# Projection and attention in one block, attention's setup among the last u products, MLP's last tile by halves

## The chip, the cores and the metric

The kernel runs on one core of one Trainium2 chip. The time is the device time of one execution in microseconds (us); of several executions the median is given. Lower is better. The five engines of a core are TensorE (PE in the rows, its weight loads PEld), VectorE (DVE), ScalarE (ACT), GpSimd (POOL) and SyncE (SP), which here only issues DMAs. They run side by side, each in its own program order, and wait for one another through semaphores.

## What is computed

One layer of a diffusion backbone, in float32, on 1024 latent tokens and 128 context tokens of width 1024:

```python
h = rmsnorm(x, norm1) * (1 + scale1) + shift1
proj = h @ w_in
q_a, kv_a, k_r, u = jnp.split(proj, [256, 384, 416], axis=-1)
q = (rmsnorm(q_a, q_norm) @ w_qb).reshape(B, S, N_HEADS, QK_DIM)      # 8 heads of 64 + 32
ckv = rmsnorm(kv_a, kv_norm)
kv = (keys_ckv @ w_kvb).reshape(B, K, N_HEADS, QK_NOPE_DIM + V_HEAD_DIM)
attn = mla_attend(q_nope, q_rope, k_nope, keys_kr, v)                 # softmax over latent and cached keys
pooled = pool_mix(u, w_pool, pool_scale)                              # windowed means of u, 4 groups
x = x + gate1 * (jnp.concatenate([attn, pooled], axis=-1) @ w_o)
h2 = rmsnorm(x, norm2) * (1 + scale2) + shift2
x = x + gate2 * (jnp.square(jax.nn.relu(h2 @ w1)) @ w2)               # 1024 -> 4096 -> 1024
```

A last `rmsnorm(x, final_norm)` gives y. Scale, shift and gate come from `silu(c) @ w_ada + b_ada`, once for the latent tokens and once for the context. ckv and the rotary key of the context tokens are outputs too.

## The kernel before

Every large product is made of three: each float32 operand is split into a high part (ScalarE, `ACT.Copy` into fp32r) and the rest (VectorE or GpSimd, a subtraction), and high·high, high·low and low·high add up in one PSUM bank. So each tile goes through PE, ACT and DVE in turn, and of the eight PSUM banks some are always being split.

The program has three blocks. At the border of two blocks all engines meet at a barrier.

**project_phase** (from L184). Nine token tiles of 128. `STEPS` numbered steps; tables such as `A_AT`, `U_AT` and `M_AT` say what each engine does at which step. `U_AT` places the 16 products `project_u` (L763, written m = 0 to 15: 4 blocks of tiles by 4 groups of columns of u), `M_AT` the products `mix` (L790) that follow them three steps later. Between these two, one m passes `read_u` on ACT, `windows` on POOL, `pooled` on DVE, `pooled_high` on ACT and `pooled_low` on DVE; after `mix`, `mixed` on ACT. The sums for the first gate (`gate_sums`, L798) multiply 128x128 weights by `sel`, which has two columns; they stand at step 26 on PE, behind the last u product (step 24) and between the last mixes. The queries' input `qnT`, the compressed keys `ckvT` and the rotary key rows `krT` are left for the next block. `small_hi` and `small_lo` make them, the context tile's last (step 24).

**attention_phase** (from L835). First a setup with nothing else beside it: the weights of heads 0 and 1 are split (L1076, L997), PE makes head 0's three key pieces (L1318) and three query pieces (L1307), then the values of all heads for ten key tiles (`V`, L1418, 30 products of 512 columns), with five banks in turn. ACT and DVE split the keys, put the rotary rows `krT` into `kT` for both buffers (L1134, L1246), turn the queries (`turn_query`, L1191), fill `ropeq` with ones (L1249) and split the values (L1144, L1257). Then a loop runs over `u` = 0 to 67: 64 units (8 heads by 8 query tiles), each with `scores(u)` (nine products of 384 columns, L1337) on PE, `maximum(u)` on DVE (L1210, L1212), `exponent(u)` on ACT (L1110) and, one to two units later, transposes (L1351) and products with `V` (L1362), four for a pair of units in flight. Sides of the loop are the next head's keys and queries (`SIDE_AT`), sums for three later modulations (`ADA_AT` on DVE and POOL, and `MOD_AT` on PE: L1381, again products by `sel`, four times in the loop) and the context's own attention. `scores(u)` for u > 0 waits until the exponent of u-1 has read the banks. Banks 0 to 2 hold scores, bank 6 the products with `V`, banks 3, 4, 5 and 7 are a ring for all the rest.

**closing_phase** (from L1511). The output projection (L1694), and then the MLP in three blocks of 3 token tiles by 32 slices of the hidden width: `up` (L1951), ReLU and square, `down_tile` (L1959). Behind the last slice PE makes the last three tiles one by one, each with 12 products of 512 columns in two banks. For each, DVE multiplies by the gate in two halves (L1900), POOL adds to x in two halves (`residual`, L1763), ACT takes the sum of squares (L1831), POOL makes the inverse root (L1767, L1769), DVE scales (`last_norm`, L1906) and SP stores (L1748).

## Time and profile before

| what | us |
|---|---|
| median of 3 runs (1518.1, 1518.25, 1522.72) | 1518.25 |
| the profiled execution | 1522.2 |
| its span, first to last instruction | 1520.4 |
| PE busy in the span | 1417.0 |
| VectorE busy | 842.6 |
| ScalarE busy | 689.1 |
| GpSimd busy | 404.0 |
| mean granted clock of TensorE, share of full speed | 0.972 |

The span is one execution on the chip. The profiled execution is 1.8 us longer than its span, and 3.95 us longer than the median. The clock of TensorE has two levels in this trace, 1.00 (2.4 GHz) and 0.50 (1.2 GHz); a mean between them says how much of a stretch stood at each. In a row of the timeline the first number is the start and the second the time that the instruction (or a run of like ones, with its count behind x) took, and in brackets stands how long its engine had been idle before it, and on what.

### The profile page before, as it was taken

How to read it: one execution, taken by the hardware profiler on the slowest of the kernel's cores; microseconds unless marked ns; L12 is line 12 of the kernel's file. 1: busy time of each engine (PE TensorE's matmuls, PEld its weight loads, DVE VectorE, ACT ScalarE, POOL GpSimd, SP SyncE). 2: the span in 40 equal slices, each digit the busy share in tenths (PEclk: the TensorE clock that was granted, in tenths of full speed). 3: DMA queues.
4: the chain of work that ended last, by engine and by line, in shares of the span. 5: the costliest groups of instructions: out<-in, count | busy, mean ns of one | idle time of the engine just before them, and what ended most of it. 6: DMA issues, size and time to landing. Idle time of an engine off the chain costs nothing.

```text
span 1520.4 us, 20734 instructions
## 1 busy us (share of the span) xinstructions
PE 1417.0 (93%) x7676; PEld 1258.7 (83%) x7676; DVE 842.6 (55%) x1237; ACT 689.1 (45%) x1382; POOL 404.0 (27%) x515
## 2 busy tenths in 40 slices
PE   5899879999889887999999999999999999999996
PEld 1698868888778886889999888899999889999995
DVE  6577467777676774425555445554444555444444
ACT  5576456566555653223333344333334434333332
POOL 3385536556565522454000000200000021000003
PEclk8799989999999998999999999999999999999998
DMA  8422011000000005015434333243333334333321
GB/s 291 153 84 65 3 50 39 15 33 33 33 29 17 27 29 207 1 42 208 166 138 163 128 130 119 111 158 132 131 118 137 112 110 166 125 135 113 138 83 42
DMA packets 46719, 152.53 MB, mean 100 GB/s; under 512 B 7256, under 2 KB 9816, under 8 KB 46648
## 3 DMA queue, kind: packets, MB, share of 16 engines
q1 hardware_dynamic: 45784, 148.47, 27.3%
q0 software_dynamic: 864, 3.15, 0.5%
q8 instruction: 41, 0.67, 0.2%
q14 instruction: 30, 0.25, 0.1%
HBM read 146.63 MB, written 4.80 MB: 100 GB/s over the span
## 4 chain that ended last, share of the span: by engine, by line
PE 58%; DVE 2%; POOL 1%; ACT 1%; DMA 0%; issue 0%; ACTq 0%; DVEq 0%; POOLq 0%
PE bank L1959 26%; PE bank L1951 25%; PE bank L1694 6%; POOL x L1763 1%; PE bank L1468 1%; DVE wol L1656 0%; DMA h2f<-in_w_o 0%; DVE w1l L1858 0%; PE bank L1499 0%; DVE add L1900 0%; PE bank L1973 0%; DVE rTl L1869 0%; DVE sq L1865 0%; DVE w2l L1858 0%; ACT rTh L1812 0%
## 5 line engine op out<-in xcount | busy, mean ns | idle before, releaser
L1951 PE MATMUL bank<-h2h,w1l 128*128 128x384 f32 x768 | 258.3, 336 | 0.0
L1951 PE MATMUL bank<-h2l,w1h 128*128 128x384 f32 x768 | 258.2, 336 | 0.0
L1951 PE MATMUL bank<-h2h,w1h 128*128 128x384 f32 x768 | 258.2, 336 | 0.0
L1763 POOL TENSOR_TENSOR x<-x,add 128x512 f32<-128x512 f32 x18 | 24.3, 1382 | 717.7 <-DVE add L1900 717.7
L1959 PE MATMUL bank<-w2h,rTh 128*128 128x512 f32 x576 | 181.9, 397 | 7.8 <-DVE rTl L1869 7.8
L1959 PE MATMUL bank<-w2l,rTh 128*128 128x512 f32 x576 | 179.0, 392 | 0.0
L1959 PE MATMUL bank<-w2h,rTl 128*128 128x512 f32 x576 | 177.9, 390 | 0.0
L1812 ACT ACTIVATE rTh<-sq 128x384 fp32r<-128x384 f32 x94 | 49.4, 525 | 242.0 <-PE bank L1959 238.1
L1801 ACT ACTIVATE relu<-bank 128x384 f32<-128x384 f32 x94 | 46.1, 490 | 247.0 <-PE bank L1951 247.0
L1869 DVE TENSOR_TENSOR rTl<-sq,rTh 128x384 fp32r<-128x384 f32 x96 | 53.6, 558 | 172.5 <-ACT rTh L1812 168.3
L1858 DVE TENSOR_TENSOR w1l<-w1raw,w1h 128x1024 fp32r<-128x1024 f32 x94 | 117.2, 1247 | 55.2 <-ACT w1h L1794 55.2
L1951 PEld LDWEIGHTS bank<-h2l,w1h 128*128 128x128 f32 x768 | 144.0, 188 | 3.9
L1951 PEld LDWEIGHTS bank<-h2h,w1h 128*128 128x128 f32 x768 | 144.1, 188 | 3.6
L1951 PEld LDWEIGHTS bank<-h2h,w1l 128*128 128x128 f32 x768 | 144.0, 187 | 0.0
L1110 ACT ACTIVATE prow<-bank,nm 128x768 f32<-128x768 f32 (+1 forms) x128 | 93.6, 736 | 94.9 <-DVE nm L1212 90.5
L1858 DVE TENSOR_TENSOR w2l<-w2raw,w2h 128x1024 fp32r<-128x1024 f32 x95 | 116.4, 1226 | 36.0 <-ACT w2h L1794 36.0
L1865 DVE TENSOR_TENSOR sq<-relu 128x384 f32<-128x384 f32 x96 | 54.5, 568 | 143.0 <-ACT relu L1801 139.2
L1203 DVE TENSOR_TENSOR plo<-bank,phi 128x512 fp32r<-128x512 f32 (+1 forms) x160 | 95.5, 630 | 64.2 <-ACT phi L1126 63.9
L1959 PEld LDWEIGHTS bank<-w2h,rTl 128*128 128x128 f32 x576 | 108.1, 188 | 24.2
L1959 PEld LDWEIGHTS bank<-w2l,rTh 128*128 128x128 f32 x576 | 108.2, 188 | 24.0
L1959 PEld LDWEIGHTS bank<-w2h,rTh 128*128 128x128 f32 x576 | 105.8, 188 | 26.6 <-issue 10.1
L1210 DVE TENSOR_REDUCE mx<-bank 128x1 f32<-128x768 f32 (+1 forms) x128 | 90.9, 749 | 28.1 <-PE bank L1337 27.9
(265 smaller groups left out, 2915.4 us busy)
## 6 DMA issues: line engine op xcount, KB each, us to landing
w1raw<-in_w SPq DMA_DIRECT2D x96, 512.0 KB, 3.5
w2raw<-in_w SPq DMA_DIRECT2D x96, 512.0 KB, 4.4
ada_raw<-in_w_ada SPq DMA_DIRECT2D x24, 512.0 KB, 4.5
xn<-in_w_ada SPq DMA_DIRECT2D x16, 512.0 KB, 3.5
xin<-in_x SPq DMA_DIRECT2D x9, 512.0 KB, 3.7
x<-in_x SPq DMA_DIRECT2D x3, 1536.0 KB, 12.1
g_raw<-in_w_ada SPq DMA_DIRECT2D x8, 512.0 KB, 3.4
out_y<-x POOLq DMA_DIRECT2D x6, 512.0 KB, 5.5
```

The lines of the kernel that those rows point to most:

```text
L1110: nc.scalar.activation(prow[:, s, lo * BN:hi * BN].rearrange("p (a b) -> p a b", b=BN), scores_in[:, lo:hi, :], ACT.Exp, bias=nm[:, s:s + ...
L1203: nc.vector.tensor_tensor(plo[i % 3][:, 0:n], ring_bank("turn", i)[:, 0:n], phi[i % 3][:, 0:n].bitcast(F32), ALU.subtract).then_inc(t_lo, 1)
L1210: nc.vector.tensor_reduce(mx[:, s, part:part + 1], scores_in[:, lo:hi, :], AX_XY, ALU.max).then_inc(nm_ready, 1)
L1694: op = nc.tensor.matmul(b[i][:, :], src[x][:, t % 2, c % 4, :], wo[y][:, c, i * 512:(i + 1) * 512], start=first, stop=last)
L1763: nc.gpsimd.tensor_tensor(k.x[:, t, cut], k.x[:, t, cut], add[:, i, :], ALU.add).then_inc(out_added, 1)
L1801: nc.scalar.activation(relu[s][:, :], bank[6 + s][:, 0:BN], ACT.Relu).then_inc(relu_done, 1)
L1812: nc.scalar.activation(rT[s][0][:, :], sq[s][:, :], ACT.Copy).then_inc(r_hi, 1)
L1858: nc.vector.tensor_tensor(w[m][slot][1][:, :], raw[m][rslot][:, :], w[m][slot][0][:, :].bitcast(F32), ALU.subtract).then_inc(w_ready[m], 1)
L1865: nc.vector.tensor_tensor(sq[s][:, :], relu[s][:, :], relu[s][:, :], ALU.mult).then_inc(sq_done, 1)
L1869: nc.vector.tensor_tensor(rT[s][1][:, :], sq[s][:, :], rT[s][0][:, :].bitcast(F32), ALU.subtract).then_inc(r_ready, 1)
L1951: op = nc.tensor.matmul(bank[6 + s][:, 0:BN], w[0][s][x][:, c * P:(c + 1) * P], k.h2[b % 2][y_][:, c, :], start=n == 0, stop=n == 3 * DC - 1)
L1959: op = nc.tensor.matmul(bank[2 * i + half][:, :], rT[s][x][:, i * P:(i + 1) * P], w[1][s][y_][:, half * 512:(half + 1) * 512], start=first ...
```

## The change

1. The first two blocks become one, `opening_phase`. Its attention buffers take the places of projection buffers in SBUF from before the block begins, so the order of their use is kept by waits: the load of `w_v` waits for `u_filled`, that of `ropeq` for `proj_ready`, the memset of `ropeq` for `proj_ready`.
2. Steps 25 to 28 go (`STEPS` is 25). Splitting head 0's and head 1's weights comes at step 23, the split of the value weights at step 24. Straight behind the last u product PE makes head 0's first query piece and its three key pieces (banks 6, 0, 1 and 3), then `mix(13)`, then the other two query pieces.
3. `scores(0)` no longer waits for the values nor for the rotary rows of head 1's buffer. Behind `scores(0)` come `gate_sums` and `mix(14)`; in u = 1 `mix(15)` and five value tiles, in u = 2 the other five. They use three banks in turn (7, 5, 6). The rotary rows of head 1's buffer are made in u = 3 (ACT) and u = 4 (DVE).
4. `ADA_AT` and `MOD_AT` stand one unit later.
5. Of the MLP's very last tile PE finishes first one half of the columns, then the other. DVE adds each half to x itself, behind its gate; ACT squares halves; POOL adds the two sums before the inverse root; DVE scales halves and SP stores halves.

The diff, cut to that (the functions that only move from `attention_phase` into the new block are left out):

```diff
-            project_phase(nc, a, k)
-            k.attn = sbr("attn", [P, H * VD // P, NTOK])
-            attention_phase(nc, a, k)
+            opening_phase(nc, a, k, sbr)
...
-        M_AT.update({25: 13, 26: 14, 27: 15})
...
-        STEPS = 29
+        STEPS = 25
...
+        ADA_AT = {3 + 15 * r // 4: r for r in range(NADA)}
+        MOD_AT = {15 * g + 17: g for g in range(NADA // 4)}
+        KEY_BANK, QUERY_BANK, VALUE_BANK = (bank[0], bank[1], bank[3]), (bank[6], bank[4], bank[5]), (bank[7], bank[5], bank[6])
+        KEY_ITEM, QUERY_ITEM = (2, 3, 4), (1, 5, 6)
+        VALUES_FREE = {2: 6 + NV - 2, 3: 6 + NV}
+        VALUES_AT = {1: range(0, 5), 2: range(5, NV)}
...
 # sync
+                for j in range(2):
+                    sp.dma_start(k.whr[j][:, :], a["w_head"][j]).then_inc(k.head_loaded[j], 16)
                 for r in range(5, DC):
                     gate_block(r)
+                sp.wait_ge(u_filled, 3 * G)
+                sp.dma_start(wvr, a["w_v"]).then_inc(wv_loaded, 16)
+                sp.wait_ge(proj_ready, T)
+                sp.dma_start(ropeq[NOPE:P, :], a["ropeq"]).then_inc(tabq_loaded, 16)
+                sp.wait_ge(sm_hi, len(turned))
+                sp.dma_start(k.krT[QK:P, :], k.krT[NOPE:QK, :]).then_inc(kr_doubled, 16)
...
 # gpsimd
+                    if s == 23:
+                        split_head(0)
+                windows(UG - 1)
+                low_query(0)
+                low_query(1)
+                split_head(1)
+                low_query(2)
...
 # scalar
+                    if s == 23:
+                        split_head(0)
+                        split_head(1)
+                    if s == 24:
+                        act.wait_ge(wv_loaded, 16)
+                        nc.scalar.activation(wv[0][:, :], wvr, ACT.Copy).then_inc(setup_hi, 1)
+                pooled_high(13)
+                read_u(15)
+                first_query(0)
+                first_key(0)
+                rope_rows(0)
+                first_key(1)
+                first_key(2)
+                high_query(0)
+                mixed(13)
+                first_query(1)
+                high_query(1)
+                first_query(2)
+                pooled_high(14)
+                high_query(2)
...
+                    if u == 1:
+                        mixed(15)
+                    late = list(VALUES_AT.get(u, ()))
+                    for v in late[:2]:
+                        high_value(v)
                     if u < NU:
                         exponent(u)
+                    if u == 0:
+                        mixed(14)
+                        pooled_high(15)
+                    for v in late[2:]:
+                        high_value(v)
+                    if u == 3:
+                        rope_rows(1)
...
 # vector
+                pooled_low(13)
                 dve.wait_ge(tabq_loaded, 16)
+                first_query(0)
+                first_key(0)
+                first_key(1)
+                rope_rows(0)
+                first_key(2)
+                first_query(1)
+                pooled(14)
+                first_query(2)
+                pooled_low(14)
+                pooled(15)
...
                     if u < NU:
                         maximum(u)
+                    if u == 0:
+                        gate_columns()
+                        pooled_low(15)
+                    for v in VALUES_AT.get(u, ()):
+                        low_value(v)
+                    if u == 4:
+                        rope_rows(1)
...
 # tensor, in scores(0)
+                            pe.wait_ge(setup_ready, 2)
+                            pe.wait_ge(setup_freed, KEY_ITEM[2])
...
+                def value(v):
+                    at = key_col({LT: CACHE, LT + 1: CTX}.get(v, v))
+                    if v >= 3:
+                        pe.wait_ge(setup_freed, 6 + v - 2)
+                    elif v == 0:
+                        pe.wait_ge(setup_ready, 1)
+                        pe.wait_ge(mix_done, UG)
+                    elif v == 1:
+                        pe.wait_ge(setup_freed, 6)
+                    else:
+                        pe.wait_ge(gain_done, 6)
...
                     if u < NU:
                         scores(u)
                     if u == 0:
-                        pe.wait_ge(setup_freed, 6 + NV)
+                        gate_sums()
+                        mix(14)
+                    if u == 1:
+                        mix(15)
+                    for v in VALUES_AT.get(u, ()):
+                        value(v)
+                    if u in VALUES_FREE:
+                        pe.wait_ge(setup_freed, VALUES_FREE[u])
...
 # closing_phase, vector, in finish
+                            if n == 2 * T - 1:
+                                dve.wait_ge(down_done, NB * FC - 2 + BLK + 1)
                             if n >= 2:
                                 dve.wait_ge(out_added, n - 1)
...
+                            if t == T - 1:
+                                dve.wait_ge(out_gated, 2 * t + 2 * i + 1)
+                                nc.vector.tensor_tensor(k.x[:, t, cut], k.x[:, t, cut], add[:, i, :], ALU.add).then_inc(out_gated, 1)
...
 # closing_phase, tensor
-                for i in range(BLK):
+                for i in range(BLK - 1):
...
+                for half in range(2):
+                    down_tile(0, BLK - 1, halves=(half,))
+                    down_tile(1, BLK - 1, last=True, halves=(half,)).then_inc(down_done, 1)
```

On PE, from the mix before the gate sums to the first scores, before (L1299 is the barrier between the blocks, L1418 a value tile, `sel` the two columns of the gate sums):

```order
L790 MATMUL bank<-pTh,wpl 128x272
L798 MATMUL bank<-sel,xn 128x2 x16
L790 MATMUL bank<-pTh,wph 128x272
...
L1299 UNCONDITIONAL_BRANCH
L1318 MATMUL bank<-ckvTh,whh 64x512
...
L1307 MATMUL bank<-qnTh,whh 128x384
...
L1418 MATMUL bank<-phi,ckvTh 128x512
L1418 MATMUL bank<-plo,ckvTh 128x512
...
L1337 MATMUL bank<-kTh,qTh 128x384
```

The same stretch of PE's program after the change (L1270 is the last u product, L1323 a query piece, L1334 a key piece, L1356 the scores, L1436 a value tile, L1297 a mix):

```order
L1270 MATMUL bank<-hTh,wul 128x256
L1323 MATMUL bank<-qnTh,whh 128x384
...
L1334 MATMUL bank<-ckvTh,whh 64x512
...
L1297 MATMUL bank<-pTh,wph 128x272
...
L1356 MATMUL bank<-kTh,qTh 128x384
...
L1305 MATMUL bank<-sel,xn 128x2 x16
...
L1436 MATMUL bank<-phi,ckvTh 128x512
```

The scores have moved ahead of the gate sums, of two mixes and of all values. On DVE, behind the last step, before (L663 reads the gate sums, L1243 splits the value weights, L1246 the rotary rows of both buffers, L1257 the values, L1210 is the first maximum):

```order
L642 TENSOR_TENSOR pTl<-total,pTh 128x272
L663 TENSOR_TENSOR mod<-bank,cols 128x8 x2
...
L1243 TENSOR_TENSOR plo<-xn,phi 128x512
L1246 TENSOR_TENSOR kTl<-krT,kTh 64x1280 x2
L1249 MEMSET ropeq 64x1152
...
L1257 TENSOR_TENSOR V<-bank,V 128x8x64 x10
L1210 TENSOR_REDUCE mx<-bank 128x1 x2
```

and after (L1015 and L1009 belong to the pooling mixer, L1042 turns a query piece, L1048 splits a key piece, L1095 the rotary rows of one buffer, L1061 is the maximum, L1107 splits values):

```order
L1042 TENSOR_TENSOR qf0<-bank,ropeq 64x384
L1048 TENSOR_TENSOR kTl0<-bank,kTh0 64x512 x2
L1095 TENSOR_TENSOR kTl0<-krT,kTh0 64x1280
L1048 TENSOR_TENSOR kTl0<-bank,kTh0 64x256
L1042 TENSOR_TENSOR qf1<-bank,ropeq 64x384
L1009 SCALAR_TENSOR_TENSOR total<-total,ub 128x272
...
L1015 TENSOR_TENSOR pTl<-total,pTh 128x272
...
L1061 TENSOR_REDUCE mx<-bank 128x1 x2
...
L1107 TENSOR_TENSOR V<-bank,V 128x8x64 x5
```

Head 0's keys and queries now share DVE with the mixer's last pieces, and the maximum of the first scores stands ahead of the values.

## Rows read from the trace of the kernel before

**Rows 1.** The page: busy time, share of span and instructions of each engine

```profile
PE 1417.0 (93%) x7676; PEld 1258.7 (83%) x7676; DVE 842.6 (55%) x1237; ACT 689.1 (45%) x1382; POOL 404.0 (27%) x515
```

**Rows 2.** Stretches: us, busy PE, PEld, DVE, ACT, POOL, PEclk, DMA share, GB/s

```profile
180.00:200.00 20.00, 13.52 (x74) 11.27 (x72) 7.91 (x14) 9.12 (x21) 5.54 (x16) 0.74 0.18 44
...
260.00:280.00 20.00, 18.54 (x131) 17.02 (x130) 15.60 (x29) 12.30 (x32) 12.73 (x18) 1.00 0.11 34
```

**Rows 3.** Timeline of PE, last u product to first scores: start us, us, what

```profile
181.07 0.28 PE L763 MATMUL bank<-hTh,wul 128*128 128x256 f32 x1
...
182.07 3.63 PE L798 MATMUL bank<-sel,xn 128*128 128x2 f32 x32
...
211.11 0.40 PE L1418 MATMUL bank<-phi,ckvTl 128*128 128x512 f32 x1
211.35 0.34 PE L1337 MATMUL bank<-kTh,qTh 128*128 128x384 f32 x1
```

**Rows 4.** Timeline of ACT over the same border

```profile
188.43 0.63 ACT L528 ACTIVATE mixT<-bank,cols 128x136 f32<-128x136 f32 x2 [1.20 <-PE bank L790]
...
194.09 2.43 ACT L1134 ACTIVATE kTh<-krT 64x1280 fp32r<-64x1280 f32 x2
196.54 1.34 ACT L1100 ACTIVATE kTh<-bank 64x512 fp32r<-64x512 f32 x3
...
201.88 0.52 ACT L1095 ACTIVATE qTh<-qf 128x384 fp32r<-128x384 f32 x1 [3.61 <-DVE qf L1191]
202.31 0.47 ACT L1081 ACTIVATE qf<-bank 64x384 f32<-64x384 f32 x1
...
214.48 0.90 ACT L1110 ACTIVATE prow<-bank,nm 128x768 f32<-128x768 f32 x1 [2.34 <-DVE nm L1212]
...
227.06 0.90 ACT L1110 ACTIVATE prow<-bank,nm 128x768 f32<-128x768 f32 x1 [1.93 <-DVE nm L1212]
```

**Rows 5.** Timeline of DVE over the same border

```profile
186.74 0.44 DVE L642 TENSOR_TENSOR pTl<-total,pTh 128x272 fp32r<-128x272 f32 x1 [1.36 <-ACT pTh L521]
...
195.40 2.89 DVE L1246 TENSOR_TENSOR kTl<-krT,kTh 64x1280 fp32r<-64x1280 f32 x2 [0.61 <-ACT kTh L1134]
...
199.64 1.61 DVE L1197 TENSOR_TENSOR kTl<-bank,kTh 64x512 fp32r<-64x512 f32 x3
201.28 0.56 DVE L1191 TENSOR_TENSOR qf<-bank,ropeq 64x384 f32<-64x384 f32 x1
...
206.11 6.76 DVE L1257 TENSOR_TENSOR V<-bank,V 128x512 fp32r<-128x512 f32 x10 [1.08 <-ACT V L1144]
212.79 1.41 DVE L1210 TENSOR_REDUCE mx<-bank 128x1 f32<-128x768 f32 x2
```

**Rows 6.** Stretches, columns as in rows 2, for the clock behind two-column products

```profile
186.00:196.00 10.00, 6.40 (x21) 4.71 (x20) 1.88 (x5) 4.95 (x10) 1.68 (x2) 0.50 0.35 88
...
300.00:305.00 5.00, 5.00 (x20) 5.00 (x21) 2.88 (x6) 1.11 (x3) 3.69 (x3) 0.50 0.00 0
...
552.00:554.00 2.00, 2.00 (x11) 1.90 (x10) 1.79 (x6) 0.00 (x0) 0.00 (x0) 0.50 0.00 0
```

**Rows 7.** Timeline of PE: the first of the loop's four modulation sums

```profile
297.49 2.43 PE L1381 MATMUL bank<-sel,xn 128*128 128x2 f32 x16 [0.92 <-DVE plo L1203]
```

**Rows 8.** Timeline of all engines at the end of the program

```profile
1506.15 2.54 POOL L1763 TENSOR_TENSOR x<-x,add 128x512 f32<-128x512 f32 x2 [0.22 <-DVE add L1900]
...
1508.16 1.29 DVE L1900 TENSOR_TENSOR add<-bank,gate 128x512 f32<-128x512 f32 x2 [1.49 <-PE bank L1959]
...
1509.63 3.46 POOL L1763 TENSOR_TENSOR x<-x,add 128x512 f32<-128x512 f32 x2
...
1513.11 1.06 ACT L1831 ACTIVATE junk<-x 128x1024 bf16<-128x1024 f32 x1 [3.24 <-POOL x L1763]
...
1516.11 1.28 DVE L1906 SCALAR_TENSOR_TENSOR x<-x,stat,fnorm 128x1024 f32<-128x1024 f32 x1 [0.76 <-POOL stat L1769]
```

**Rows 9.** DMA issues at the end: KB each, median us from issue to landing

```profile
out_y<-x SPq DMA_DIRECT2D x3, 512.0 KB, 2.6
```

925 lines of the change are left out of this document (462 added, 463 removed).

## The prediction

> **What bounds the kernel now.** The page's busy times come first: TensorE is busy 93% of the span, VectorE 55%, ScalarE 45% [rows 1]. So a microsecond is won only where TensorE waits or runs at the low clock. The stretches show where: from 180 to 200 us it is busy 13.52 of 20 at a mean clock of 0.74, while from 260 to 280, well inside the attention loop, it is busy 18.54 of 20 at 1.00 [rows 2]. The timelines of one engine over that border say why. The last u product starts at 181.07 and the first scores at 211.35 [rows 3]; in these 30 us stand the last mixes, a barrier, head 0's keys and queries, and 30 value products, with each hand-over between PE, ACT and DVE exposed. The second place is the end. There PE is done at about 1508.1, and DVE, POOL, ACT, POOL, DVE and a store follow one another until 1520.4 [rows 8]. The MLP between is dense and is not touched.
>
> **Part 1, the first scores come earlier.** I follow the order of the new program with the durations of the old one. At full clock, start to start, a product of 512 columns takes 0.24 us (from the last value product to the first score) [rows 3]; by columns that is 0.18 for 384 and 0.12 for 256.
> - PE: the last u product ends at 181.35 [rows 3]. The weights of head 0 are split at step 23, within ACT's and POOL's waits there, so I count nothing for them; they would cost 0.9 us if that cover were gone (ACT is put back by two such splits before the context tile's `small_hi`). The query piece takes 6 x 0.18, to 182.5, the three keys 6 x 0.24 + 3 x 0.12, to 184.3.
> - ACT from 182.5: the query's upper rows 0.47, key 0 0.55 (behind PE), the rotary rows 2.43 / 2, key 1 0.55, key 2 0.3, the query's high part 0.52 [rows 4]: to 186.2. The rotary copy DMA is issued behind the last `small_hi`, near 180, and is there by then.
> - DVE: query 0.56, key 0 0.6 (to 184.5), key 1 behind ACT at 185.6 to 186.3, the rotary rows 2.89 / 2 to 187.8, key 2 0.4 [rows 5]: 188.2. POOL's low part of the query is ready before that.
>
> So `scores(0)` starts at 188.2 instead of 211.35, 23.1 us earlier. If DVE never waited, its pieces alone (about 5.3 us behind 180.3) would allow 185.6; if each hand-over cost 0.1 more it would be 189.5.
>
> **Part 2, what was taken out comes back in u = 0 to 2.** The gate sums took 3.63 us on PE before [rows 3], the values 30 x 0.24 = 7.2 on PE and 6.76 on DVE [rows 5], each mix 0.4 on PE with 0.44 on DVE and 0.63 on ACT [rows 4, 5], and one buffer's rotary rows 1.2 and 1.45. Before the first maximum DVE still owes two query pieces, `pooled` twice and `pooled_low`: 0.56 x 2 + 0.44 x 3, with ACT between, to 191.3. The maximum and its scalar take 1.6: exponent 0 starts at 192.9 (before: 214.48 [rows 4]).
> - u = 0: PE makes the scores to 189.8, gate sums to 193.3, the mix and head 1's first key to 194.4, scores 1 to 196.0. Exponent 0 (0.90 for the first piece [rows 4], 1.6 with the shorter second) ends at 194.5; ACT's `mixed` and `pooled_high` and DVE's `pooled_low(15)` follow to 196.0. So DVE has maximum 1 at 197.6.
> - u = 1: exponent 1 stands behind `mixed(15)` (197.1) and two values (PE 0.72 each, ACT 0.6 each): 199.1 to 200.7. Three values follow on ACT; DVE splits five (0.68 each) and a key, to 203.9, then has maximum 2 at 205.5.
> - u = 2: exponent 2 at 205.5 to 207.1, three values on ACT, DVE has the last of them at 209.8. PE waits for the eighth, turns, and makes scores 3 to 210.5; then DVE has a low part and maximum 3: exponent 3 starts at 212.3.
>
> Before it started at 227.06 [rows 4]. At a full clock that is 14.8 us won. The rotary rows of the second buffer (1.45 on DVE, 1.2 on ACT, in u = 3 and 4) stand ahead of low parts that PE waits for; DVE had about a microsecond free there, so I take 0.5 (0 to 1.45): 14.3. The modulation's sums move by one unit, from beside idle time to beside idle time: nothing.
>
> **Part 3, the clock.** Behind the gate sums the clock stood at 0.50 from 186 to 196, though a mix and the key products ran. The loop has four more such groups of products by `sel`, half as long [rows 7], and behind three of them it fell as well, while PE stayed busy: 300 to 305 and 552 to 554 are the first and the last [rows 6]. In the new program 3.5 us of gate sums follow some 1.4 us of idle and 1.6 us of scores, and denser work only begins behind them. I expect the low level from about 193.5 to 200. On the path to exponent 1 stand then a key, scores 1, a mix and two values, 0.7 + 1.6 + 0.4 + 1.4 = 4.1 us of full-speed work that takes twice that; about 1.1 is covered by ACT and DVE at `pooled_low(15)`. Cost: 3.0. Part 1 to 3: **11.3 us**. Ends: 0 (the clock holds) and 6 (it stays low through u = 2, with the values at 1.4 us each).
> The Trainium skill, "TensorE: Matmul & The Clock Gate", section "Why this matters for your kernels", says that speed is kept as long as no idle gaps lie between bursts of matmuls. The new stretch has no gap as long as those before, so by this rule the clock would hold and the sum would be 14.3. The rows 6 speak against it: at 300 to 305 PE was busy all five microseconds.
>
> **Part 4, the end.** Now POOL adds the last tile in 3.46 us, where the tile before took 2.54, behind two gates of 0.65 each; x is complete at 1513.09 [rows 8]. After: PE finishes the first half at 1506.7, 6 x 0.24 before its end. DVE's first gate must wait until POOL has added the first half of tile 7 (1507.4), and then gate, add, gate, add, 4 x 0.7, end at 1510.3. ACT squares the halves to 1511.4; POOL's add and power come behind (I estimate 0.9 to 1.5 from the 2 us between the last square's end and the last scaling's start, which hold POOL's two pairs), beside DVE's scalings of tiles 6 and 7, 1.28 each, which run on to 1512.9. The halves are scaled by 1513.6 to 1515. Each store of 512 KB lands 2.6 us after its issue [rows 9], and at the end before it came from 1517.4 to 1520.4. Four stores now start between 1511.6 and 1515; in sequence, at the 1.7 us that 512 KB need in the present flow, they end at 1517.8. Won: **2.6 us** (1.5 if POOL's small instructions wait out both scalings, 3.6 if they don't and the stores overlap). The adds moved to DVE cost it 1.4 us, with nothing queued behind but scalings that wait for POOL anyway.
>
> **The sum.** 11.3 + 2.6 = 13.9. Against the profiled execution that is 1522.2 - 13.9 = 1508.3, a span of 1506.5. That execution is 3.95 above the median of the three runs, and I don't know by which dip of the clock; against the median it is 1518.25 - 13.9 = **1504.4**.
>
> **Rivals.**
> 1. The clock holds (or falls where nothing waits for PE). For it: the stretch is denser than before. Against it: three of four. 14.3 + 2.6: 1501.4.
> 2. The values' three banks become the wait. Every value needs PE, ACT and DVE in turn, 0.72 + 0.6 + 0.68 = 2.0, over three banks 0.67 each, which is no more than DVE's own pace; but exponents and maxima stand in ACT's and DVE's order between them, and PE's next scores are queued behind the values. If each of u = 1 and 2 loses another 2.5 us, 11.3 becomes 6.3: 1509.4.
> 3. It does not do what it says at the front: head 0's weights or the rotary copy arrive late and `scores(0)` starts no earlier than 200, as where the three engines' programs wait in another order than I read. 11.9 us less: the whole is a gain of 2: 1516.3.
> 4. Slower: the low clock stays. Each microsecond of PE work at 0.50 costs one more. From the gate sums on, 14.3 + 2.6 us of full-speed work at half clock, about all of u = 0 to 4, cancels the change; double that, to u = 7, makes 1535. No low stretch with a busy PE in rows 6 is over 5 us, so this needs a new pattern.
>
> **Chances.** Forecast 0.5, rival 1 0.22, rival 2 0.18, rival 3 0.06, rival 4 0.04. The range takes forecast, rival 1 and rival 2: from 1499.5 (rival 1 with the end's 3.6 and a dip less) to 1510. About 0.3%, 4.6 us, is what a measurement of this kernel tells from no change. Faster by more: forecast and rivals 1 and 2 save for a margin, 0.91; within: 0.06; slower: 0.03.
>
> **What would show it.** In the profile after: first scores near 188, the exponents 0 and 3 near 193 and 215; the clock at 0.50 in the stretch behind the gate sums; PE waiting for DVE's value splits less than a microsecond each; from 260 on the same rows as before, 11 us earlier; x of the last tile complete at 2 us behind PE's last product instead of 5; the last store issued about 6 us behind PE's end instead of 9.3. The forecast is wrong if the first scores come later than 191, if exponent 3 comes before 213 or behind 218, or if the attention loop's later dips of the clock change in number.

## The result, and the profile after

The changed kernel took 1511.78 us (median of 4 runs, 1508.72 to 1512.74), the kernel before 1520.49 beside it (4 runs, 1518.10 to 1522.79): a ratio of 0.9938, with a 95% interval of 0.9924 to 0.9952. A later group of 6 runs gave 1512.03 against 1522.88, 0.9924 (0.9899 to 0.9950). The forecast was 1504.4 in a range from 1499.5 to 1510.0: the kernel is faster as foretold, by too little. A ratio, here and below, is not that of the two medians beside it; the two can differ by 0.1%. The 58 runs of the kernel before that stand beside the experiments have a median of 1521.44 (all 75 on record: 1521.35), the 11 of the changed one 1511.6, so the gain is 9.8 us where 13.9 were forecast.

The profiled execution of after took 1512.74 us with a span of 1510.8. Its page gives busy time, share of the span and instructions of each engine; TensorE (PE) has 5.9 us less than in [rows 1], with as many instructions, at a mean clock of 0.978 instead of 0.972:

```profile
PE 1411.1 (93%) x7676; PEld 1257.9 (83%) x7676; DVE 843.3 (56%) x1240; ACT 689.4 (46%) x1384; POOL 403.8 (27%) x514
```

The stretches, columns as in [rows 2] (busy us of PE, PEld, DVE, ACT, POOL, then the granted clock), of after:

```profile
180.00:200.00 20.00, 17.75 (x82) 16.33 (x81) 11.20 (x18) 10.12 (x25) 9.61 (x17) 0.71 0.12 38
260.00:280.00 20.00, 18.64 (x126) 16.61 (x124) 15.61 (x30) 13.45 (x35) 11.81 (x18) 1.00 0.11 36
188.00:203.00 15.00, 14.27 (x58) 13.44 (x56) 6.92 (x13) 5.04 (x14) 3.74 (x5) 0.54 0.11 35
```

From 180 to 200 PE is now busy 17.75 us instead of 13.52, as intended, but at a clock of 0.71. The third row shows why: 15 us at 0.54, full of work. Multiplied out, 15 x (1 - 0.54) = 6.9 us of full speed were lost here. The timeline of PE in after, last u product, first scores, the gate's sums, and the first wait in u = 1:

```profile
179.68 0.28 PE L1270 MATMUL bank<-hTh,wul 128*128 128x256 f32 x1
...
187.50 0.41 PE L1356 MATMUL bank<-kTh,qTh 128*128 128x384 f32 x1 [2.25 <-POOL qTl L579]
...
189.72 6.82 PE L1305 MATMUL bank<-sel,xn 128*128 128x2 f32 x32
...
203.08 0.47 PE L1436 MATMUL bank<-phi,ckvTh 128*128 128x512 f32 x1 [0.81 <-ACT mixT L756]
```

The sums that took 3.63 us in [rows 3] take 6.82. ACT in after: exponents 0, 1 and 3, and behind the last the second buffer's rotary rows ahead of two high parts:

```profile
193.21 0.90 ACT L803 ACTIVATE prow<-bank,nm 128x768 f32<-128x768 f32 x1 [3.51 <-DVE nm L1063]
...
205.24 0.89 ACT L803 ACTIVATE prow<-bank,nm 128x768 f32<-128x768 f32 x1
...
218.08 0.90 ACT L803 ACTIVATE prow<-bank,nm 128x768 f32<-128x768 f32 x1 [1.92 <-DVE nm L1063]
...
219.66 1.27 ACT L823 ACTIVATE kTh<-krT 64x1280 fp32r<-64x1280 f32 x1
220.95 1.09 ACT L819 ACTIVATE phi<-bank 128x512 fp32r<-128x512 f32 x2
```

Exponent 0 (193.21) comes 1.7 us later, counted from the last u product, than the forecast had it. VectorE (DVE) in after, ahead of it, with three instructions of the mixer, and POOL beside the last two:

```profile
187.57 0.44 DVE L1009 SCALAR_TENSOR_TENSOR total<-total,ub 128x272 f32<-128x272 f32 x1
...
189.17 1.15 DVE L1015 TENSOR_TENSOR pTl<-total,pTh 128x272 fp32r<-128x272 f32 x1
190.24 1.23 DVE L1009 SCALAR_TENSOR_TENSOR total<-total,ub 128x272 f32<-128x272 f32 x1
```
```profile
189.14 0.87 POOL L565 TENSOR_TENSOR whl<-whr,whh 128x320 fp32r<-128x320 f32 x1
189.97 1.20 POOL L579 TENSOR_TENSOR qTl<-qf,qTh 128x384 fp32r<-128x384 f32 x1
```

The forecast had 0.44 for each. The first, with POOL idle from 187.36 to 188.18, took 0.44; the two beside POOL took 1.15 and 1.23, which is 1.5 of the 1.7 us, and it is the same within 0.02 in after_third, e3_gate_ahead and e12_query_first. No experiment took POOL's two instructions away from there.

Behind exponent 3 comes what the forecast had hardly priced. PE in after waits three times in u = 4 to 6 (the number in brackets):

```profile
222.32 1.03 PE L1370 MATMUL bank<-ident,prow 128*128 128x128 f32 x6 [1.37 <-DVE plo L1054]
...
227.21 0.63 PE L1370 MATMUL bank<-ident,prow 128*128 128x128 f32 x4 [2.44 <-DVE kTl L1048]
...
238.88 1.09 PE L1389 MATMUL bank<-ident,rs 128*64 128x128 f32 x8 [1.16 <-DVE clo L1222]
```

PE in a second trace of the kernel before (before_again) waits there once for over 0.3 us, 0.60 us for the same key part (0.78 in before):

```profile
229.97 0.63 PE L1351 MATMUL bank<-ident,prow 128*128 128x128 f32 x4 [0.60 <-DVE kTl L1197]
```

DVE over the same time in after has the 1.49 us of rotary rows directly ahead of the key's low part (0.68) and, in u = 6, the modulation's two products (1.75) ahead of the context tile's low part (0.28), which is what PE waits for:

```profile
224.86 1.49 DVE L1095 TENSOR_TENSOR kTl<-krT,kTh 64x1280 fp32r<-64x1280 f32 x1
226.38 0.68 DVE L1048 TENSOR_TENSOR kTl<-bank,kTh 64x512 fp32r<-64x512 f32 x1
...
236.87 1.75 DVE L1082 SCALAR_TENSOR_TENSOR xn<-xn,sf 128x512 f32<-128x512 f32 x2
238.55 0.28 DVE L1222 TENSOR_TENSOR clo<-bank,chi 128x128 fp32r<-128x128 f32 x1
```

The end, all engines of after, to hold against [rows 8]:

```profile
1500.17 0.40 PE L2042 MATMUL bank<-w2h,rTl 128*128 128x512 f32 x1
...
1502.32 0.69 DVE L1977 TENSOR_TENSOR x<-x,add 128x512 f32<-128x512 f32 x1
...
1503.22 0.63 ACT L1921 ACTIVATE junk<-x 128x512 bf16<-128x512 f32 x1
...
1503.17 1.45 POOL L1829 TENSOR_TENSOR stat<-stat,nhalf 128x1 f32<-128x1 f32 x1
1504.70 1.31 POOL L1846 TENSOR_SCALAR stat<-stat 128x1 f32<-128x1 f32 x1
...
1506.97 1.42 DVE L1985 SCALAR_TENSOR_TENSOR x<-x,stat,fnorm 128x512 f32<-128x512 f32 x2 [1.03 <-POOL stat L1851]
```

x of the last tile is complete at 1503.01, 2.4 us behind PE's end (1500.57), where the forecast had 2.2. ACT's squares are done at 1503.85; then GpSimd's (POOL's) one-column instructions, 0.57 us when alone, take 1.45 and 1.31 beside DVE's scalings. From PE's end to the end of the span: 12.3 us before, 10.2 after.

**One ruler for all traces.** The phases ahead of the border hold dips of the clock that differ from run to run, so traces are compared from the end of the last u product (its start plus 0.28). "Lost" is the sum of (1 - granted clock) over the border, about 30 us behind it; the old opening loses part of it while PE idles. The last column is the same sum from 25 to 15 us ahead of that end, so before the border begins: some executions have a low stretch there and some have not.

| trace | exponent 0 | exponent 3 | exponent 8 | lost, us | lost ahead of it |
|---|---|---|---|---|---|
| before, before_again, before_third | 33.1, 32.3, 32.0 | 45.7, 45.1, 44.7 | 71.8, 71.2, 70.8 | 8.5, 6.8, 6.8 | 1.7 each |
| e2_tail (old opening) | 33.8 | 46.3 | 72.4 | 8.5 | 0 |
| after, after_again | 13.3, 13.2 | 38.1, 38.0 | 68.3, 68.3 | 6.8, 6.8 | 1.7 each |
| after_third | 13.2 | 33.4 | 63.7 | 1.7 | 0 |
| e1_front (same opening) | 13.2 | 33.3 | 64.8 | 1.7 | 0 |
| e3_gate_ahead | 13.2 | 32.6 | 62.8 | 1.7 | 0 |
| e4_gate_one (14 of 16 sums left out) | 13.2 | 35.8 | 66.0 | 5.1 | 0 |
| e5_gate_u3 | 13.2 | 34.7 | 68.8 | 5.1 | 1.7 |
| e11_fill | 13.2 | 34.9 | 66.3 | 3.4 | 1.7 |
| e7_rope | 13.2 | 38.2 | 66.1 | 6.8 | 1.7 |
| e8_gate_rope | 13.2 | 32.7 | 60.6 | 1.7 | 0 |
| e9_gate_rope_ada | 13.2 | 32.7 | 59.3 | 1.7 | 0 |
| e10_ada_one | 13.2 | 32.7 | 59.3 | 1.7 | 0 |
| e12_query_first | 13.7 | 38.3 | 68.5 | 6.8 | 1.7 |

### The profile page after: what moved, and what is told of

Read it like the earlier page. It is cut to its first block, busy times and chain, and to the rows that moved or that the text cites. A ratio compares the mean times of both kernels' runs of the same rounds, so it can differ in the third digit from the quotient of the medians.

```text
span 1510.8 us, 20733 instructions
## 1 busy us (share of the span) xinstructions
PE 1411.1 (93%) x7676; PEld 1257.9 (83%) x7676; DVE 843.3 (56%) x1240; ACT 689.4 (46%) x1384; POOL 403.8 (27%) x514
## 4 chain that ended last, share of the span: by engine, by line
PE 58%; DVE 2%; POOL 1%; ACT 1%; DMA 0%; issue 0%; DVEq 0%; ACTq 0%; POOLq 0%
PE bank L2042 26%; PE bank L2034 25%; PE bank L1750 6%; POOL x L1823 1%; PE bank L1524 1%; DVE wol L1712 0%; DMA h2f<-in_w_o 0%; DVE w1l L1929 0%; PE bank L1555 0%; DVE add L1973 0%; PE bank L2056 0%; DVE rTl L1940 0%; DVE sq L1936 0%; DVE w2l L1929 0%; ACT rTh L1878 0%
## 5 line engine op out<-in xcount | busy, mean ns | idle before, releaser
L1823 POOL TENSOR_TENSOR x<-x,add 128x512 f32<-128x512 f32 x16 | 20.9, 1339 | 717.7 <-DVE add L1973 717.7
L1061 DVE TENSOR_REDUCE mx<-bank 128x1 f32<-128x768 f32 (+1 forms) x128 | 91.0, 750 | 28.1 <-PE bank L1356 27.3
## 6 DMA issues: line engine op xcount, KB each, us to landing
x<-in_x SPq DMA_DIRECT2D x3, 1536.0 KB, 12.5
```

Of the source, the lines that this page charges most:

```text
L1061: nc.vector.tensor_reduce(mx[:, s, part:part + 1], scores_in[:, lo:hi, :], AX_XY, ALU.max).then_inc(nm_ready, 1)
L1823: nc.gpsimd.tensor_tensor(k.x[:, t, cut], k.x[:, t, cut], add[:, i, :], ALU.add).then_inc(out_added, 1)
```

## The experiments

**The two halves of the change.** e1_front has the new opening and the old closing block; e2_tail the old opening and the new closing block.

> The new border between projection and attention, with the old closing block (last tile of the MLP as before). The whole change gave 9.4 us at the medians. In the trace of after, 10.2 us lie between TensorE's end and the end of the span, 12.3 before, so the closing's part should be 2.1 and this kernel should be 7.3 us faster than before: near 1513 (ratio 0.9952). If instead the front's gain is all lost in the attention loop, it comes out within 2 us of before.

> The old border, with the new closing block alone. Forecast on record for this part: 2.6 us. From the two traces: 2.1 us faster than before (near 1518.2). If the halves' extra instructions only move the wait to GpSimd's small instructions, less than 1.

e1_front: 1512.64 against 1521.97, ratio 0.9946 (0.9926 to 0.9966), 8.2 us by the ratio. e2_tail: 1517.47, 0.9977 (0.9965 to 0.9990), 3.5 us with an interval from 1.5 to 5.3. In the traces PE's end lies 12.3 us ahead of the span's end in e1_front as in before, and 10.3 in e2_tail; the tail's part is 2.1. Both expectations lie within the intervals. Unlooked for, e1_front's opening, which is that of after, started exponent 3 4.8 us sooner than after's.

**The gate's sums.** e3_gate_ahead:

```
                 project_query(2, QUERY_BANK[2], setup_filled)
+                pe.wait_ge(setup_freed, 1)
+                gate_sums()
...
                     if u == 0:
-                        gate_sums()
                         mix(14)
```

> After, with the gate's column sums ahead of the first scores (where TensorE idled 2.25 us at 185.25 to 187.5) instead of behind them. Theory A (the sums at the low clock, 6.8 us ahead of scores 1, ate the gain): the sums run at the full clock in 3.6 us, the first scores start at 188.9 instead of 187.5, scores 1 start 4 to 5 us earlier, and the whole is 2 to 4 us faster than after. Theory B (not the sums but the hand-overs of the values and maxima between TensorE, ScalarE and VectorE in u = 1 and 2): exponent 3 stays at 218 within 1 us and the time stays within 1 us of after. Theory C: the low clock follows the sums wherever they stand; then scores 0 and 1 take 3.2 us each, and nothing is won.

PE in e3_gate_ahead: the sums stand in the former wait at the full clock, and the first scores start as soon as they end.

```profile
184.12 3.63 PE L1305 MATMUL bank<-sel,xn 128*128 128x2 f32 x32
187.60 0.42 PE L1356 MATMUL bank<-kTh,qTh 128*128 128x384 f32 x1
```

The sums now put the first scores back by 1.0 us (8.6 instead of 7.5 behind the last u product, 8.9 expected) instead of standing 6.8 us behind them. Exponents 1, 3 and 8 come 5.5 us earlier than in after. The median is 1510.02, ratio 0.9927 (0.9913 to 0.9941): 1.6 us below after's first ratio (0.9938) and 0.5 above its second (0.9924), which the intervals don't tell apart. The trace bears out theory A against this one trace of after. Against after_third (below), the changed kernel itself with the same 1.7 us lost, exponents 3 and 8 come only 0.8 and 0.9 us earlier: that is what moving the sums gave where the clock fell alike. And exponent 0 comes at 13.2 in both, though the first scores start a microsecond later: it waits for VectorE's order and not for them.

e4_gate_one leaves 14 of 16 sums out (`for c in range(1)`), so the gate that it computes is not the right one.

> After, with 2 of the gate's 16 column sums computed and 14 left out (the modulation's gate columns are then wrong; 28 of 32 passes fewer on TensorE). It prices the sums. Theory A: exponent 1 starts 6 us earlier (near 199), exponent 3 near 212.5, and the whole is 5 to 6 us faster than after. Theory B: exponent 3 gains under 2 us since the values' hand-overs hold it. If the ramp behind it has room that takes up any gain (theory E), exponent 3 gains 5 but exponent 8 less than 1.5 and the time less than 2.

Exponent 3 gained 2.3 us, not 5 or 6; median 1509.63, ratio 0.9925 (0.9911 to 0.9939). So the sums alone are not worth 5 us. The stretches of e4_gate_one show what took their place: hardly any sums, and yet 11 us at 0.53.

```profile
188.00:193.00 5.00, 2.94 (x18) 2.28 (x16) 4.36 (x6) 1.29 (x4) 3.00 (x3) 1.00 0.31 105
193.00:204.00 11.00, 8.96 (x25) 7.62 (x26) 3.85 (x9) 6.18 (x17) 0.75 (x2) 0.53 0.00 0
```

**The same program again.** after_again and after_third are the changed kernel, before_again and before_third the one before.

> The changed kernel once more, unchanged, for a second trace and a second median. The same opening code took the clock's fall at 188.3 us in the trace of after and at 194.3 in that of e1_front, so that the gate's sums took 6.82 us in one and 3.63 in the other. Theory A' (the moment of the fall is not set by the code): here it lies anywhere between 185 and 196, the sums take between 3.6 and 6.8 us, and exponent 3 starts between 33 and 38.5 us behind the last u product. If the sums themselves made the clock fall, they take 6.8 again. In either case the ramp from exponent 3 to exponent 8 takes 30.2 us within 1.5 and TensorE waits 1.3 us for plo and 2.4 for the key's low part in it, and the median lies within 1.5 us of 1511.8.

> The changed kernel once more, for its trace alone. In four traces of this opening the low clock took 6.8 us at the border in three and 1.7 in one; here either, with the gate's sums at 6.8 or 3.6 us and exponent 3 at 38.0 or 33.3 us behind the last u product, and the ramp from exponent 3 to 8 at 30.2 in both (31.4 if a low stretch falls into it).

The first repeated after's border to 0.1 us (6.8 lost, sums 6.8). The second did not; PE and the border's stretch in after_third:

```profile
189.81 3.63 PE L1305 MATMUL bank<-sel,xn 128*128 128x2 f32 x32
```
```profile
188.00:203.00 15.00, 13.98 (x75) 11.97 (x76) 8.72 (x16) 8.11 (x21) 3.90 (x7) 0.89 0.10 35
```

Same code, same 2.25 us wait ahead of the scores, but the clock falls at 194.1 instead of 188.5, and 1.7 us are lost instead of 6.8; exponent 3 comes 4.6 us sooner and the run took 1507.93. So the size of the border's loss is not a property of the code alone: of this opening two traces of four (five of seven with e7_rope, e12_query_first and e11_fill counted) lost 3.4 or more.

The two executions already differ ahead of the changed place. Their stretches, first after, then after_third, some 20 us ahead of the last u product's end:

```profile
156.00:164.00 8.00, 7.63 (x52) 7.65 (x53) 4.47 (x13) 4.96 (x16) 5.24 (x7) 0.79 0.13 35
```
```profile
156.00:164.00 8.00, 5.78 (x46) 5.53 (x47) 4.40 (x10) 5.61 (x21) 4.64 (x6) 1.00 0.12 37
```

The table's last column has this for all traces, and for those whose program is the same up to the fall at the border (but for one instruction's place in e12_query_first), it sorts them without an exception: after, after_again, e7_rope and e12_query_first have the low stretch there and lost 6.8, after_third and e1_front have it not and lost 1.7. It is six traces and no experiment sets it, so it shows what goes together and not what causes it. The times of the changed kernel fall into two groups as well: 4 of its 11 runs took 1506.5 to 1508.7 us at a mean clock of 0.982 to 0.984, the other 7 took 1511.3 to 1517.6 at 0.974 to 0.978, and the three traced ones lie in the group that their border's loss says. A median of few runs depends on how many of each it holds.

The 58 runs of before, 1516.6 to 1525.8 us, go with their mean granted clock too (correlation -0.79, 0.9 us for each 0.001).

> The kernel before as it is, for a second trace of the old opening and for what two groups of runs of one program differ by. By the terms that five traces of the new opening repeat, the change is worth 5.6 us (3.5 at exponent 8, 2.1 in the tail); the medians say 9.4 and 10.9. If the rest is in how often the low clock falls elsewhere, this trace has the same waits as that of before (ramp from exponent 3 to 8 in 26.1 us, the first TensorE waits of the border 1.19 and 2.41 us) with another number of low stretches, and its time goes with the microseconds lost to them: near 1515 with 36 lost, near 1521 with 42. If there is a term in the work itself that the comparison of the two traces missed, two traces of before agree on it. The median lies within 1.5 us of the other runs of before.

> The kernel before once more, for its trace alone: see before_again.

before_again: 1520.49 (12 runs), ratio 1.000 (0.9988 to 1.0012). The three traces of the old opening agree within 1.0 us at exponents 3 and 8, and their ramps take 26.1 us each. With e2_tail's they put exponent 8 at 71.6 on average; after, after_again, after_third and e1_front at 66.3. That is 5.3 us, with the tail 7.4, and it is what the same eight traces' spans differ by (7.5 with the tail's 2.1 evened out). The runs that happened to be traced were thus among before's faster ones, and the traces ask for no further term in the work. The 2.4 us to the medians' 9.8 are within what runs of one program differ by (9 us in before, 11 in after); more than that isn't shown.

**What brings the low stretch.** e11_fill puts 12 unused products into the wait; e5_gate_u3 moves the sums to u = 3.

```
+                for _ in range(12):
+                    nc.tensor.matmul(bank[2][:, 0:BN], wh[0][0][:, 0:P], k.qnT[0][:, 0, 0:BN], start=True, stop=True)
```

> After, with 12 products of 384 columns (about 2.1 us, into a bank that the first scores overwrite) in the place where TensorE idles 2.25 us ahead of the first scores; their result is used by nothing. The sums stay behind the scores. In three of four traces of this opening the border lost 6.8 us to the low clock, which began 7.5 to 8.9 us behind the last u product; with the sums ahead of the scores it lost 1.7 in three of three. Theory G (what helped there was that the idle stretch was filled): the border's loss falls to 1.7, the sums take 3.6 to 5, exponent 3 starts 33 to 34 us behind the last u product, and the median is 3 to 4.5 below after's. Theory H (what helped was that the two-column sums no longer stand behind the scores, near the fall): the clock falls as in after, the sums take 6.8 us, exponent 3 starts at 38 and the median is after's within 1.5.

> After, with the gate's sums in u = 3, behind the last value, and their reading on VectorE there too. The idle 2.25 us ahead of the first scores stays. Theory H: with no sums near the fall the low clock is left after 3.4 us as in e3_gate_ahead, exponent 3 starts near 33 to 34 us behind the last u product, and the sums cost 3.6 us in u = 3: the median is 1 to 2.5 below after's. Theory G (the idle stretch decides): the low stretch is as long as in e4_gate_one, where only 4 of the 32 passes were left (5.1 us lost), exponent 3 starts near 36, and with 3.6 us for the sums in u = 3 the median is after's or 1 us above.

PE in e11_fill and its stretches:

```profile
187.79 0.41 PE L1356 MATMUL bank<-kTh,qTh 128*128 128x384 f32 x1 [0.19 <-POOL qTl L579]
189.43 4.87 PE L1305 MATMUL bank<-sel,xn 128*128 128x2 f32 x32
```
```profile
188.00:203.00 15.00, 14.14 (x70) 12.67 (x70) 8.32 (x15) 7.09 (x17) 3.73 (x5) 0.77 0.11 36
```

The wait is down to 0.19, the fall comes at 191.6, 3.4 us are lost instead of 6.8. Neither theory is met: exponent 3 at 34.9 lies between, and the time didn't move (1512.27, 0.9933, 0.9907 to 0.9959); a low stretch from 225 to 229, which after doesn't have, took 1.2 of it back by exponent 8. e5_gate_u3 took 1514.82, 0.9956 (0.9942 to 0.9971), by the ratios 2.7 us above after (0.9938; 4.9 against 0.9924): the border lost 5.1 as theory G says, exponent 3 at 34.7 lies between the two, and the sums took 4.44 us in u = 3, with another low stretch there. So neither the idle wait nor the two-column sums are shown as the cause. With the sums ahead, four traces of four (e3, e8, e9, e10) lost 1.7. But all four are also executions without the low stretch ahead of the border, and the changed kernel lost 1.7 in those too: whether the place of the sums does anything to the clock is not shown. Of the executions with that stretch, e11_fill lost 3.4 and e5_gate_u3 5.1 where four others lost 6.8, one trace each.

**The rotary rows of the second buffer.** e7_rope moves ScalarE's copy from u = 3 to the end of u = 1, VectorE's subtraction from u = 4 to the end of u = 3.

```
# ScalarE
-                    if u == 3:
+                    if u == 1:
                         rope_rows(1)
...
# VectorE, ahead of the low parts
-                    if u == 4:
-                        rope_rows(1)
...
# VectorE, behind ada_latent
+                    if u == 3:
+                        rope_rows(1)
```

> After, with the second buffer's rotary rows moved: ScalarE's copy from the end of u = 3 to the end of u = 1, VectorE's subtraction from u = 4 (ahead of a key's low part) to the end of u = 3, where it stood idle 2.36 us. Theory F (these two instructions, 1.27 and 1.49 us ahead of work that TensorE waits for, cost the ramp): TensorE's waits of 1.34 (plo, u = 4) and 2.43 us (key's low part, u = 5) shrink to under 0.2 and 0.8, the ramp from exponent 3 to 8 takes 27 to 27.6 us instead of 30.2, and the median is 2.5 to 3.5 us below after's, if the clock falls alike. Rival (the ramp waits for its first probabilities anyway, and a hand-over later in it takes the slack): the ramp still takes 29.5 to 30.2.

PE in e7_rope, the two waits again:

```profile
224.44 1.03 PE L1370 MATMUL bank<-ident,prow 128*128 128x128 f32 x6 [0.55 <-DVE plo L1054]
...
227.68 0.63 PE L1370 MATMUL bank<-ident,prow 128*128 128x128 f32 x4 [0.79 <-DVE kTl L1048]
```

The waits fall by 2.5 us and the ramp from exponent 3 to 8 from 30.2 to 27.9; the median is 1509.31, ratio 0.9910 (0.9892 to 0.9928). In the traces theory F holds, with 0.3 to 0.9 us less than expected; the ratio is not told apart from after's 0.9924 beside it. The missing part: in e8_gate_rope, which has the same edit, VectorE's subtraction runs from 215.71 to 217.20 and the next low part starts at 217.23, so it is not quite free.

**Both, and the modulation's table.** e8_gate_rope has the edits of e3_gate_ahead and e7_rope; e9_gate_rope_ada and e10_ada_one add to it:

```
# e9_gate_rope_ada
-        ADA_AT = {3 + 15 * r // 4: r for r in range(NADA)}
-        MOD_AT = {15 * g + 17: g for g in range(NADA // 4)}
+        ADA_AT = {(2 + 15 * r // 4 if r else 3): r for r in range(NADA)}
+        MOD_AT = {15 * g + 16: g for g in range(NADA // 4)}
...
# e10_ada_one
-        ADA_AT = {3 + 15 * r // 4: r for r in range(NADA)}
+        ADA_AT = {(5 if r == 1 else 3 + 15 * r // 4): r for r in range(NADA)}
```

> The two edits together: the gate's column sums ahead of the first scores (as in e3_gate_ahead) and the second buffer's rotary rows moved (as in e7_rope). Both theories: exponent 3 starts 32.6 us behind the last u product, exponent 8 at 59.8 to 60.3 instead of 62.8 (e3) and 68.3 (after), and the median is 1507 within 1.5. If the two edits win the same wait, it is e3's 1510.

> As e8_gate_rope, and the modulation's steps (its loads, partial products and sums) back in the units of the kernel before, all but the first of the sixteen. In e3's trace TensorE waited 1.16 us for the context tile's low part, which stood behind two of these partial products (1.75 us) on VectorE in u = 6, and 0.3 for GpSimd. If that shift cost this, exponent 8 comes 1.0 to 1.4 us earlier than in e8_gate_rope and the median 1 to 1.5 lower, near 1505.7. Rival: the same two products then delay another low part, in u = 5, and nothing changes.

> e8_gate_rope, with only the second of the modulation's 16 steps moved one unit earlier (from u = 6 to u = 5) and all others, and their sums, left. In e8 TensorE waited 1.25 us for the context tile's low part behind this step's two products on VectorE; in e9_gate_rope_ada, where all steps and sums were one unit earlier, that wait was gone and exponent 8 came 1.3 us earlier, but the units 16 and 17 took 2.7 us more. Expected: both gains at once, exponent 8 at 59.2 to 59.3 behind the last u product, units 9, 14, 16, 17 as in e8, and a median 1.0 to 1.3 below e8's 1504.9. Rival: the slack is taken up by the unit at the next wait, and only e8's time is reached.

e8_gate_rope: 1504.86, 0.9886 (0.9866 to 0.9905), that is 18.0 us below before's 1522.88 beside it and 6.8 below the changed kernel's 1511.6; exponent 8 at 60.6 is 7.8 us sooner than in after, and 3.1 sooner than in after_third, where the clock fell alike: 0.8 from the sums' place and 2.3 from the rotary rows. Of the 6.8 us the edits are shown to give these 3.1; the rest is clock or not explained. Expected were 59.8 to 60.3 and 1507 within 1.5: the time is a little better than that. e9_gate_rope_ada: exponent 8 1.3 sooner, as expected, yet the median is 1507.03, 0.9899 (0.9880 to 0.9917). The intervals don't tell the two apart, but the traces differ at the first of the loop's modulation sums, PE in e9_gate_rope_ada and in e8_gate_rope:

```profile
284.90 1.92 PE L1400 MATMUL bank<-sel,xn 128*128 128x2 f32 x16 [0.90 <-DVE plo L1054]
```
```profile
291.26 1.84 PE L1400 MATMUL bank<-sel,xn 128*128 128x2 f32 x16
```

In unit 16 (the old table, [rows 7]) they wait 0.9 us, in unit 17 not at all. Behind them the clock falls in e9 (286 to 291 us, 1.7 lost, PE busy 5.00 of 5) and stays up in e8. All five traces with the old table have this low stretch, and two of the twelve with the new one (e1_front and e11_fill, where the two units take 12.5 us). The units 16 and 17 take 14.05 us in e9, 13.6 to 15.1 with the old table in before and e2_tail, and 11.3 in e8 and after. e10_ada_one has exponent 8 at 59.3 and those units at 11.3, both as expected, and a median of 1504.98, 0.9898 (0.9879 to 0.9917): not told apart from e8's, so the last 1.3 us are shown in the trace and not in the time.

**A small instruction beside VectorE.**

```
                 first_key(0)
+                high_query(0)
                 rope_rows(0)
                 first_key(1)
                 first_key(2)
-                high_query(0)
```

> After, with ScalarE's high part of the first query piece ahead of its rotary rows. GpSimd's low part of that piece (128 x 384) took 2.20 us in after, beside VectorE's rotary rows (128 rows of the page's 64 x 1280, both operands in SBUF), and 1.01 for the next piece. If the two slow each other, the low part, now done before VectorE's rotary rows begin, takes 1.0 us, and the first scores start 7.3 to 7.5 us behind the last u product's end instead of 7.55, held by VectorE. If the first of these low parts is slow for another reason, it takes 2.2 again.

POOL in after, and in e12_query_first:

```profile
185.16 2.20 POOL L579 TENSOR_TENSOR qTl<-qf,qTh 128x384 fp32r<-128x384 f32 x1 [0.69 <-ACT qTh L788]
```
```profile
186.60 1.01 POOL L579 TENSOR_TENSOR qTl<-qf,qTh 128x384 fp32r<-128x384 f32 x1
```

Out of the way of VectorE's rotary rows (185.01 to 186.50 in after) it takes 1.01 us. It wins nothing: VectorE's key parts come later by as much, and the first scores start 7.7 us behind the last u product instead of 7.5, now with 2.39 us of wait for the key's low part (expected 7.3 to 7.5).

The Trainium skill ("GPSIMD Engine Reference", section "1. Specifications") states that GpSimd shares its SBUF interfaces with VectorE and contends with VectorE instructions that have two SBUF inputs; the pair 2.20 and 1.01 agrees.

## Why the prediction was wrong, point by point

The two steps that failed are the clock behind the gate sums (part 3: 3.0 us; measured 6.8 or 1.7 lost) and what follows exponent 3 (the end of part 2: 0.5 us; measured 4.5). Averaged over four traces each of the old opening and of the new one, exponent 3 comes 9.8 us sooner, where part 1 to 3 without the 0.5 had 11.8; from there to exponent 8 the new opening takes 30.6 us and the old one 26.1, so 4.5 us are given back where the forecast had 0.5. The second failure is the larger (4.0 of 6.0 us), stands in every trace of the changed opening (30.2 to 31.4 us), and is mostly accounted for by e7_rope (2.3) and by e9 and e10 (1.3).

- **The first scores** (188.2): 187.50, or 7.54 us behind the last u product where the sum had 6.85. Right in kind, and the scores waited for POOL's low part of the query (2.20 us), which the sum had ready in time. VectorE's last key part was done at 186.95, so POOL put them back by 0.55. It cost nothing further on, as the next point shows.
- **u = 0 to 2**: exponent 0 came 13.2 us behind the last u product, forecast 11.6. Exponent 3 without a low clock was put at 31.0; after_third with 1.7 lost has 33.4. The step was 0.7 to 2.4 us too short. The late start of the scores is not the reason: exponent 0 comes at 13.2 in e3_gate_ahead too, whose scores start 1.0 later. Between them stand VectorE's two instructions of 1.15 and 1.23 us that the sum had at 0.44. The three steps from exponent 0 to 3 were put at 6.2, 6.4 and 6.8 without a low clock, and take 7.4, 6.4 and 6.4 in after_third with its 1.7 lost in the first of them: that part came out about as put.
- **The clock** (cost 3.0, from 193.5 to 200): this is the term that failed most in the trace on which the change was read. The fall came at 188.5, ahead of the sums and not behind them, and 6.8 us were lost with PE busy 14.27 of 15 us, 0.8 beyond the end of 6 that was kept for it. The sum had priced the gate's sums at 3.63 and only the work behind them at the low level. In after_third the same term is 1.7, under the 3.0. Part 3 took the fall as following from the order of the work; which of the two losses an execution has goes with a low stretch 20 us earlier, which no term of the sum looked at. Exponent 3 at 218.08 met the text's own mark for "wrong" (behind 218); in after_third it starts at 214.1, inside it.
- **The rotary rows of the second buffer** (0.5, ends 0 and 1.45): 2.35 us are regained by moving them alone (e7_rope's ramp). The step counted VectorE's instruction once. In fact each engine's copy stood ahead of a part that PE waited for, in different units, and the waits added: 1.37 and 2.44 us instead of none and 0.6 to 0.8.
- **The modulation's table** (nothing): 1.3 us lost in u = 6 (removed in e9 and e10) and about 2.5 us regained in units 16 and 17 (14.1 us on average with the old table, 11.6 in the four traces of the changed opening). The words "from beside idle time to beside idle time" were wrong twice. The gain doesn't show over the loop: exponents 8 to 63 take 302.6 to 307.2 us before and 304.7 to 307.1 after, with low stretches at other places.
- **The tail** (2.6; ends 1.5 and 3.6): 2.1. The order of events was as foretold; two of POOL's small instructions, 1.45 and 1.31 us, end 0.1 to 0.4 behind the VectorE scaling beside which they ran.
- **The base.** The sum was set against 1518.25, the median of three runs, and the text said it did not know by which dip the profiled run was slower. Before's median over 58 runs is 1521.44, so the base was 3.2 us low by the luck of three runs. From 1521.44 the same sum gives 1507.5 and the same range ends at 1513.2, beyond the measured 1511.78: with another base the same faulty terms would have met the range. By gains the forecast is 4.1 us too high: by the averaged traces the opening gives 5.3 at exponent 8 instead of 11.3 at exponent 3, the tail 2.1 instead of 2.6, and 2.4 of the medians' 9.8 are left over.
- **Rivals.** Rival 1 (the clock holds) was seen in no trace: every one of the seventeen has a low stretch at the border. The Trainium skill's rule in "TensorE: Matmul & The Clock Gate", section "Why this matters for your kernels", that speed is kept without long idle gaps between bursts, would give that rival. The stretches of e3_gate_ahead speak against it: PE is busy in every microsecond from 180 to 191, and the clock is at 0.50 from 188.9 on (it is idle only in the last part of the second stretch):

```profile
184.00:188.00 4.00, 4.00 (x36) 4.00 (x35) 3.31 (x6) 2.21 (x7) 3.00 (x2) 1.00 0.00 0
...
189.00:192.00 3.00, 2.72 (x9) 1.49 (x7) 2.93 (x5) 0.00 (x0) 1.19 (x2) 0.50 0.39 149
```

Rival 2 named about the right size (6.3 us at the front) but a wrong place: PE's waits for VectorE's values are 0.8 and 0.2 us in after. Rivals 3 and 4 didn't come.

What stays open is what sets the moment at which the clock falls, and with it whether the border loses 1.7 or 6.8 us in a given run. The low stretch 20 us earlier foretells it in the traces, but what brings that one is open too.

## What to carry to other kernels

When setup work is spread into a loop's first rounds, look for who stands right behind each moved instruction on its own engine: two copies of 1.3 and 1.5 us cost 2.4, and putting them where their engines idled won that back. Narrow products in an existing wait of TensorE rather than behind it won 0.8 us where the clock fell alike; that they keep the clock up there isn't shown. Price work next to a border at both clock levels, since one program can meet either. A base from three runs can be 3 us off here: forecast the difference, and check it on several traces of both kernels before explaining the last microseconds. Before an edit is given credit for another clock, look whether the two executions were already different ahead of it.

## What the runs showed of the hardware

- The granted clock (0.50 is the lower of its two levels, 1.2 against 2.4 GHz) fell at 188.5, 189.0 and 194.1 us in three executions of one program whose first scores started within 0.7 us of each other (187.50, 188.02, 188.15). The first two had a low stretch some 20 us ahead of the last u product's end, the third had not.
- The clock was at 0.50 with TensorE busy in every microsecond, from 188.9 to 191 in e3_gate_ahead and from 300 to 305 in before ([rows 6]).
- 32 passes with two columns took 3.63 us at the full clock and 6.82 at the low one, 1.9 times as long.
- POOL's 128x384 subtraction of two SBUF operands took 2.20 us beside VectorE's 64x1280 one and 1.01 alone, in after and e12_query_first; a one-column instruction of 0.57 us took 1.45 beside a VectorE scaling.
- The other way round, VectorE's instructions on 128x272 took 0.44 us with POOL idle and 1.15 and 1.23 beside POOL's 128x320 and 128x384 subtractions (after; 1.13 to 1.24 in after_third, e3_gate_ahead and e12_query_first).
